# First phase of a two-block transformer kernel: an embedding chunk's split ahead of the pair sums, shift rows around the sum of squares, latents' weights taken earlier

## What is computed

```python
mod = c_act @ w_ada[l] + b_ada[l]
shift, scale, gate = jnp.split(mod, 3, axis=-1)
h = rms_norm(x) * (1.0 + scale[:, None, :]) + shift[:, None, :]
proj = h @ w_in[l]
xr, gr, qc, kvc, kr, ga = jnp.split(proj, split_points(IN_SPLITS), axis=-1)
...
x = x + jax.nn.sigmoid(x @ w_ple_gate[l]) * (p[l] @ w_ple[l])      # second block
```

## Time and profile before

| | us |
|---|---|
| median of 3 runs (lowest to highest) | 2465.32 (2462.7 to 2466.88) |
| the profiled execution | 2466.83 |
| its span, first to last instruction | 2465.3 |
| TensorE busy in it | 2400.5 (97%) |
| VectorE / ScalarE / GpSimd busy | 936.3 / 834.1 / 1001.6 |
| mean granted clock of TensorE | 0.99 |

### The profile page before, as it was taken

One profiled execution on the slowest core, in us unless ns is written; L12 is line 12 of the kernel. 1 busy time (PEld: TensorE's weight loads), 2 busy tenths in 40 slices (PEclk: granted clock), 3 DMA queues, 4 the chain that ended last, 5 costly groups with the idle time before them and its releaser, 6 DMA issues.

```text
span 2465.3 us, 28183 instructions
## 1 busy us (share of the span) xinstructions
PE 2400.5 (97%) x11076; PEld 1902.2 (77%) x11076; DVE 936.3 (38%) x1485; ACT 834.1 (34%) x1283; POOL 1001.6 (41%) x434
## 2 busy tenths in 40 slices
PE   6899999999999999999999999999999999999996
PEld 4567677777888888887787778787878888888885
DVE  7744456566500520210555534343421412202113
ACT  5344444442322432222434333333322312213321
POOL 3344323234455534443332324242434444444553
PEclk8999999999999999999999999999999999999998
DMA  8952133335544343333222323232333444453332
GB/s 322 407 203 79 60 122 109 108 107 188 156 152 141 126 161 96 88 101 90 66 85 61 95 81 107 86 110 83 107 96 101 154 147 129 130 169 119 93 103 85
DMA packets 98579, 309.48 MB, mean 126 GB/s; under 512 B 10640, under 2 KB 12048, under 8 KB 98320
## 3 DMA queue, kind: packets, MB, share of 16 engines
q1 hardware_dynamic: 98448, 307.69, 38.9%
HBM read 285.63 MB, written 20.97 MB: 124 GB/s over the span
## 4 chain that ended last, share of the span: by engine, by line
PE 88%; DVE 5%; ACT 2%; issue 2%; DMA 2%; SPq 1%; POOL 0%; DVEq 0%; ACTq 0%; POOLq 0%
PE bank L539 24%; PE bank L542 24%; PE bank L540 24%; PE bank L535 2%; PE bank L538 2%; PE bank L536 2%; PE bank L1055 2%; PE bank L1079 1%; PE bank L1067 1%; DVE hlo L1756 1%; DMA rawx<-in_wst 1%; PE bank L841 1%; PE bank L852 1%; DVE hlo L2479 1%; PE bank L882 1%
## 5 line engine op out<-in xcount | busy, mean ns | idle before, releaser
L2547 POOL TENSOR_TENSOR wlo<-raw,whi 128x1024 fp32r<-128x1024 f32 x365 | 898.8, 2468 | 1217.3 <-ACT whi L1172 1191.4
L539 PE MATMUL bank<-hhi,whi 128*128 128x512 f32 x2752 | 1087.8, 395 | 14.3 <-DVE hlo L1773 8.1
L542 PE MATMUL bank<-hhi,wlo 128*128 128x512 f32 x2752 | 1078.7, 392 | 23.5 <-POOL wlo L2547 23.4
L540 PE MATMUL bank<-hlo,whi 128*128 128x512 f32 x2752 | 1076.1, 391 | 0.0
L539 PEld LDWEIGHTS bank<-hhi,whi 128*128 128x128 f32 x2752 | 518.4, 188 | 140.0 <-issue 19.4
L542 PEld LDWEIGHTS bank<-hhi,wlo 128*128 128x128 f32 x2752 | 518.5, 188 | 139.7 <-POOL wlo L2547 29.4
L540 PEld LDWEIGHTS bank<-hlo,whi 128*128 128x128 f32 x2752 | 518.7, 188 | 106.9 <-issue 0.7
L1172 ACT ACTIVATE whi<-raw 128x1024 fp32r<-128x1024 f32 x365 | 384.6, 1055 | 589.6 <-PE bank L542 483.9
L2355 DVE TENSOR_SCALAR S<-S,sm 128x512 f32<-128x512 f32 (+1 forms) x64 | 78.1, 1220 | 0.6
L538 PE MATMUL bank<-wlo,hhi 128*128 128x512 f32 x192 | 74.8, 390 | 0.8 <-POOL wlo L2547 0.8
L1621 ACT ACTIVATE S<-S,sm 128x512 f32<-128x512 f32 (+1 forms) x64 | 35.3, 551 | 119.1 <-DVE sm L2345 119.1
(11 more groups left out here) (311 smaller groups left out, 2154.0 us busy)
## 6 DMA issues: line engine op xcount, KB each, us to landing
raw<-in_wst SPq DMA_DIRECT2D x397, 512.0 KB, 3.6
rawx<-in_wst SPq DMA_DIRECT2D x54, 512.0 KB, 8.1
rawy<-in_wst SPq DMA_DIRECT2D x26, 512.0 KB, 4.6
tgs<-TS SPq DMA_DIRECT2D x32, 256.0 KB, 4.1
axr<-tgs SPq DMA_DIRECT2D x32, 256.0 KB, 4.0
X<-in_xt SPq DMA_DIRECT2D x4, 1024.0 KB, 14.4
pls<-stg SPq DMA_DIRECT2D x16, 256.0 KB, 6.5
axr<-in_xt SPq DMA_DIRECT2D x16, 256.0 KB, 2.8
```

What stands on the lines that cost most here:

```text
L539: e.matmul(o, hi, xh, start=first, stop=False)
L540: e.matmul(o, hi, xl, start=False, stop=False)
L542: return e.matmul(o, lo, xh, start=False, stop=last)
L2547: e.tensor_tensor(sub(wlo, PAIR[c], CH), slots[slot(c)], sub(whi, PAIR[c], CH).bitcast(F), ALU.subtract).then_inc(*up("wlo_pool", "wlo", c))
```

## The change

The order in `OPENING` is written anew for the front: the blocks of an embedding chunk are items of their own (`pleb`), the four `ada` chunks of group 0 stand two before and two after the sum of squares, and the first `cols` inside the third embedding chunk. In groups 1 to 7 `cols` comes three units earlier, and two of group 7's units move. A chunk `wq` becomes an item of its own, put in front of the place of its first unit by four chunks of `adt` or `ada`; the splits go one chunk ahead instead of three. GpSimd takes the first two splits before the pair sums. ScalarE makes tiles h after the shift rows of the same group, one tile after the other; VectorE makes the second half of the angles after group 0's scales, and roots x tiles between shift and lower halves. SP loads 22 instead of 19 chunks ahead of the third embedding's stores, and the second part of the constants after the stream's next part.

```diff
--- before.py
+++ after.py
@@ -49,23 +49,33 @@
 
 
 
-    out = [("ple", 0), ("ple", 1), ("xsum",), ("ple", 2)]
-    for e in range(8):
+
+    def rows(e, j):
+        return [("adt", e, j), ("ada", e, j)]
+
+    def blocks(*ns):
+        return [("pleb", n) for n in ns]
+
+    out = [("ple", 0), *blocks(1, 2, 3), ("ple", 1), *blocks(5, 6, 7), *rows(0, 0), *rows(0, 1), ("xsum",),
+           *rows(0, 2), *rows(0, 3), ("ple", 2), *blocks(9), ("cols", 0), *blocks(10, 11),
+           ("ple", 3), *blocks(13, 14, 15)]
+    for e in range(1, 8):
         u = 14 * (e - 1)
         for j in range(4):
-            out.append(("adt", e, j))
-            out.append(("ada", e, j))
-            for _ in range((0, 3, 4, 4)[j] if 0 < e < 7 else (0, 2, 2, 2)[j] if e else 0):
+            out.extend(rows(e, j))
+            for _ in range((0, 3, 4, 1)[j] if e < 7 else (0, 2, 3, 1)[j]):
                 out.append(("unit", u))
                 u += 1
-        if e == 0:
-            out.append(("ple", 3))
         out.append(("cols", e))
-        if e == 0:
-            out.append(("plelast",))
-        else:
-            out.extend(("unit", v) for v in range(u, 14 * e))
+        out.extend(("unit", v) for v in range(u, 14 * e))
     out.extend(("unit", v) for v in range(98, 112))
+    for m in range(14):
+        at = out.index(("unit", 8 * m))
+        ahead = 4
+        while ahead and out[at - 1] != ("pleb", 15):
+            at -= 1
+            ahead -= out[at][0] in ("adt", "ada")
+        out.insert(at, ("wq", m))
     return out
 
 
@@ -98,8 +108,8 @@
             out.append(("ple", item[1], 0))
         elif item[0] in ("adt", "ada"):
             out.append(item)
-        elif item[0] == "unit" and item[1] % 8 == 0:
-            out.append(("wq", item[1] // 8, 0))
+        elif item[0] == "wq":
+            out.append(("wq", item[1], 0))
     blocks("win1", range(23, 25), 2)
     blocks("uq", [4, 5, 0, 1, 2, 3], 1)
     blocks("ukvk", range(4), 1)
...
-NSTART = 1 + max(c for c, w in enumerate(PLAN) if w[0] == "wq")
+NSTART = PLAN.index(("win1", 23, 0))
...
-        return 0 if now["use"] < 2 else 3 if now["use"] < NSTART else LOOK
+        return 0 if now["use"] < 2 else 1 if now["use"] < NSTART else LOOK
...
         elif item[0] == "unit":
-            if item[1] % 8 == 0:
-                begin(c)
             if item[1] % 8 == 7:
                 end(INDEX["wq", item[1] // 8, 0])
+        elif item[0] == "wq":
+            begin(c)
     for c in range(now["use"], len(PLAN)):
...
-                if u % 8 == 0:
-                    wq["c"] = chunk("wq", u // 8, 0)
-                c, hi, lo = wq["c"]
+                c, hi, lo = wq[u // 8]
...
             for item in OPENING:
                 if item[0] == "ple":
-                    embedding(item[1], range(4) if item[1] < 3 else range(2))
-                elif item[0] == "plelast":
-                    embedding(3, range(2, 4))
+                    embedding(item[1], 0)
+                elif item[0] == "pleb":
+                    embedding(*divmod(item[1], 4))
+                elif item[0] == "wq":
+                    wq[item[1]] = chunk("wq", item[1], 0)
...
-                for whole in range(2):
-                    for k in range(2 * g, 2 * g + 2):
+                for k in range(2 * g, 2 * g + 2):
+                    for whole in range(2):
                         w.wait_ge(*done("xr", k))
                         w.wait_ge(*done("adt", INDEX["adt", g, 3]))
...
+            def shift_rows(g):
+                w.wait_ge(*done("used", INDEX["ada", g, 3]))
+                if g >= 2:
+                    w.wait_ge(*done("adacol", g - 2))
+                e.activation(RW[g % 2][:, :], bank("adarow", g)[:, 0:256], ACT.Copy).then_inc(
+                    *up("evac_act", "adacopy", g, frees=("adarow", g)))
+
             for item in OPENING:
-                if item[0] in ("ple", "adt", "ada") or item[0] == "unit" and item[1] % 8 == 0:
+                if item == ("ple", 2):
+                    w.wait_ge(*done("xsum"))
+                    w.wait_ge(*done("eps"))
+                    e.activation(rsx[:, :], bank("xsum")[:, :], ACT.Sqrt, scale=1.0 / 2048, bias=epsc).then_inc(
+                        *up("root_act", "xroot", frees=("xsum",)))
+                    shift_rows(0)
+                if item[0] in ("ple", "adt", "ada", "wq"):
                     use()
                 if item == ("ple", 0):
                     c_tanh(0)
@@ -1258,32 +1280,20 @@
                     x_squares(0, 8)
                     embedding(range(4))
                     x_squares(8, 16)
-                elif item == ("ple", 2):
                     embedding(range(4, 8))
-                    w.wait_ge(*done("xsum"))
-                    w.wait_ge(*done("eps"))
-                    e.activation(rsx[:, :], bank("xsum")[:, :], ACT.Sqrt, scale=1.0 / 2048, bias=epsc).then_inc(
-                        *up("root_act", "xroot", frees=("xsum",)))
-                elif item == ("adt", 0, 0):
+                elif item == ("pleb", 9):
+                    embedding(range(8, 10))
+                elif item == ("pleb", 11):
+                    embedding(range(10, 12))
+                elif item == ("ple", 3):
+                    h_uppers(0)
+                elif item == ("pleb", 15):
+                    embedding(range(12, 16))
+                elif item == ("adt", 1, 0):
                     sines()
-                elif item == ("adt", 0, 2):
-                    embedding(range(8, 12))
-                elif item == ("plelast",):
-                    embedding(range(12, 14))
-                    h_uppers(0)
-                    embedding(range(14, 16))
-                elif item[0] == "adt" and item[1] and item[2] == 0:
-                    if item[1] > 1:
-                        h_uppers(item[1] - 1)
-                elif item[0] == "cols":
-                    g = item[1]
-                    w.wait_ge(*done("used", INDEX["ada", g, 3]))
-                    if g >= 2:
-                        w.wait_ge(*done("adacol", g - 2))
-                    e.activation(RW[g % 2][:, :], bank("adarow", g)[:, 0:256], ACT.Copy).then_inc(
-                        *up("evac_act", "adacopy", g, frees=("adarow", g)))
-                    if g == 7:
-                        h_uppers(7)
+                elif item[0] == "cols" and item[1]:
+                    shift_rows(item[1])
+                    h_uppers(item[1])
 
 
             def x_read():
@@ -1872,26 +1882,27 @@
                 step(hba, V("b_rg_a", 0, 8), 0.5, None, ALU.mult)
                 step(hbx, V("b_rg_x", 0, 8), 0.5, None, ALU.mult, ALU.bypass, "terms")
 
-            def angles():
-                w.wait_ge("pos", 16)
-                e.tensor_copy(PF[:, :], PI32[:, :]).then_inc(*up("term_dve"))
-                step(PF[:, :], PF[:, :], V("invf"), None, ALU.mult)
+            def angles(n):
...
-                    step(KK[:, :], PF[:, :], 1.0 / (2 * np.pi), turn, ALU.mult, ALU.add)
-                    step(KK[:, :], KK[:, :], MAGIC, None, ALU.add)
...
+                        rooted_x(range(2, 4))
+                        h_lowers(0)
+                        rooted_x(range(4, 6))
                     elif g > 1 and j == 0:
                         shifts(g - 1)
-                    elif g > 1 and j == 1:
+                        rooted_x(range(2 * g + 2, min(2 * g + 4, 16)))
                         h_lowers(g - 1)
                     elif (g, j) == (1, 2):
                         w.wait_ge(*done("trig", 0))
                         step(SIN[:, :], SIN[:, :], V("sgn"), None, ALU.mult)
                         T.place["rope",] = T.place.get(("trig", 1), ("vec", 0))
                         T.place["sin",] = now("term_dve")
-                elif item[0] == "cols":
-                    g = item[1]
-                    rooted_x(range(6) if g == 0 else range(2 * g + 4, min(2 * g + 6, 16)))
-                    if g == 0:
-                        shifts(0)
-                        h_lowers(0)
             shifts(7)
             h_lowers(7)
 
@@ -2559,13 +2570,13 @@
                     w.wait_ge(*a)
                 e.tensor_tensor(HT[k][1], src, HT[k][0].bitcast(F), ALU.subtract).then_inc(*up("lo_pool", "hlo", st, k))
 
-            use()
+            use(2)
             for i in range(8):
                 w.wait_ge(*done("xsq", 2 * i))
                 w.wait_ge(*done("xsq", 2 * i + 1))
                 e.tensor_tensor(sqs[i][:, :], sqs[i][:, :], sqt[i % 4][:, :], ALU.add).then_inc(
                     *up("ssum_pool", "xpair", i))
-            use(NSTART - 1)
+            use(NSTART - 2)
             halves(SPLIT_EARLY[turn["use"]])
 
             def latent(which, hi, lo, st):
...
             embedded(0)
             embedded(1)
-            load(19)
+            load(22)
             embedded(2)
             load(24)
             embedded(3)
+            load(INDEX["win1", 24, 1] + 6)
```

(31 more changed lines are left out.)

33 lines of the change are left out of this document (21 added, 12 removed).

## The result

| | before | after |
|---|---|---|
| median, all runs on this chip (lowest to highest) | 2464.15 (2462.7 to 2466.88), 4 runs | 2444.62 (2443.56 to 2446.15), 4 runs |
| the profiled execution, its span | 2466.83, 2465.3 | 2446.15, 2444.4 |
| start of the latents' sum of squares (`sqa`), the phase's end | 179.9 | 156.7 |

The change is 19.5 us faster: ratio 0.992, 95% interval 0.9903 to 0.9937. Forecast was 2441, with a range of 2436 to 2453.

A forecast was written before the change was run, and what follows sets the result against it. The first phase was taken as bound by TensorE's waits on GpSimd's lower weight halves, with queue supply hidden behind. Terms 10.6 + 4.3 + 1.6 - 0.7 + 0 + 6.2 + 3.7 - 0.6 = 25.1 us gave 2441, range 2436 to 2453.

The forecast's parts named there:

- Step 1: Front: with the second embedding chunk split ahead of the pair sums, TensorE ends its products at 23.6 instead of 38.86 us.
- Step 2: Front: the sum of squares starts at 29 instead of 38.86 us, group 1 at 50.5; gain 10.6 us.
- its 56: Upper bound in us for the front's end, if GpSimd stretches VectorE's second half of the angles as before.
- The slow clock, taken at 1.8 us: Front: allowance of 1.8 us for TensorE's lower clock after some 5 us of idle time, slowing the sum of squares.
- Step 3: Latents' chunks four ahead, split one ahead: waits of groups 2, 5, 6 go; gains 6.2 + 3.7 us, group 1 4.3.
- The lateness of `W4` and `W11`: Groups 3 and 7: these splits, queued behind `h_uppers` on ScalarE, come 0.8 to 1.3 us late; losses 0.7 and 0.6.
- Step 4: Columns three units earlier, x tiles rooted between shift and lower halves: `hlo` waits of some 0.3 us go, counted elsewhere.
- Step 5: Load supply: no queue dip at 40 to 60 us, 0.5 us of waiting in group 2, which gains 1.6 us.
- A: Rival: the load supply binds through group 4, so the gain is only 18.9 us, giving 2446; chance 0.17.
- B: Rival: taking chunks ahead does nothing as ScalarE still splits late; only the front's gain stays, 2455; chance 0.13.
- C: Rival: slower, VectorE becomes the bound by sharing with GpSimd, 18.2 us a group, 2474; chance 0.03.
- A VectorE busy above 12 us a group: Sign in the groups of the first phase that was to prove the forecast wrong.

The follow-up runs named there:

- experiment 10: The changed kernel with the sum of squares ahead of `ada` 0,0 and 0,1 on TensorE: 2443.81 us (0.9913).
- experiment 1: The kernel before, with only GpSimd's split of the second embedding chunk moved ahead of the pair sums: 2456.39 us (0.9963).
- experiment 7: The changed kernel with columns and shift rows three units later, where they were before the change: 2443.77 us (0.9915).
- experiment 4: The changed kernel with the second half of the angles, the sines and their sign step behind the last tiles h: 2444.02 us (0.9914).
- experiment 5: As experiment 4, with the third and fourth embeddings' stores behind 36 and 46 loads instead of 22 and 24: 2445.46 us (0.992).
- experiment 11: The changed kernel with all angles behind the last tiles h, blocks 12 to 14 evacuated first, splits three ahead from chunk 80: 2451.57 us (0.9946).
- experiment 12: The changed kernel with all angles behind the last tiles h, blocks 12 to 14 evacuated first, and the sum of squares first: 2452.12 us (0.9946).
- experiment 2: The kernel before, with only the latents' chunks taken four ahead and their splits one ahead of use: 2458.33 us (0.9973).
- experiment 3: The changed kernel without the lead: latents' chunks back at their first unit, splits three ahead: 2451.67 us (0.9947).
- experiment 8: The changed kernel with splits asked three ahead from chunk 80 on; no instruction changed, so another profile of the changed kernel: 2444.55 us (0.9915).
- experiment 9: The changed kernel itself, unedited, measured and profiled a second time: 2444.77 us (0.9915).

## Why the prediction was right, by its steps

**Step 1, right.** The second embedding chunk's products run without a wait to 23.0 (23.6 said), with 0.5 us of waiting in the second profile; moving the split alone gave 12.9 us at group 1's start and 11.6 at the phase's end.

**Step 2, right in size: 10.4 us, 9.2 in the second profile, for 10.6.** The sum started at 29.85 (29 said). The reason was half right: the sum does not set the front, as experiment 10 shows; loads do, and the slow clock behind the waits for them. Nor are two `ada` chunks ahead of the sum what gives the gain: experiment 1, with the old order there, starts group 1 2.6 us earlier than the changed kernel. VectorE's chain (two rooted tiles done at 47) was the risk that the step named with its 56: they were done at 50.2 in the first profile and at 45.9 in the second. The slow clock, taken at 1.8 us, is seen in the sum, which took 8.36 us in the first profile and 9.12 in the second. The stretch of 30 to 40 us of the first:

```profile
30.00:40.00 10.00, 10.00 (x36) 4.46 (x37) 9.39 (x14) 3.76 (x5) 2.79 (x1) 0.88 1.03 407
```

and of the second:

```profile
30.00:40.00 10.00, 10.00 (x32) 4.15 (x32) 9.39 (x14) 2.87 (x3) 2.34 (x1) 0.78 1.03 408
```

**Step 3, the core, right.** Groups 5 and 6 gained 6.5 and 4.1 us (6.2 and 3.7 said). The lateness of `W4` and `W11` (-0.7, -0.6) did not come. I let `h_uppers` end 1 us into the group; ScalarE's timeline has the last one of group 2's tiles end 1 us ahead of group 3's start at 83.0, with the splits right behind:

```profile
81.33 0.80 ACT L1231 ACTIVATE un<-X,sm 128x512 f32<-128x512 f32 x1
82.03 1.04 ACT L1181 ACTIVATE whi<-rawx 128x1024 fp32r<-128x1024 f32 x1
```

GpSimd's half is done at 86.4, before the fifth unit at 87.7. Columns three units earlier moved the tiles too, which that term left out. It was too large besides: in experiment 7, with the columns late, the tiles do end 1.1 us into group 3, and GpSimd's half is done at 85.5, when the fifth unit's product with it is due at 85.6. Groups 3 and 7 gained 0.4 and 0.6 us instead of losing 1.3.

**Step 4, no term.** Experiment 7 puts it at 0.4 us in each of groups 3 to 6, and has group 2 shorter without it.

**Step 5, the term that was mis-sized.** No dip came, and the stall of group 2 for a load was foreseen, but at 0.5 us. It is 2.1 us in the second profile, and the slow clock behind it (0.90) makes group 2 16.7 us for 13.7: a loss of 1.3 against before, where 1.6 of gain stood. The step's formula had the awaited chunk (number 26, the second `ada` of group 2) land at 64.7; TensorE got it at 67.6. By the rates of that profile (365 GB/s to 40 us, 412 to 52, 410 after) some 25.9 MB had moved by then, an estimate, where the formula counts 24.8 up to that landing. What the 1.1 MB between them are no view shows; transfers already under way behind the chunk would be such. In the first profile group 2 costs the same by another way: group 1 gained 1.6 of the 4.3 said, since VectorE met two splits. Groups 1 and 2 together: 32.3 and 29.6 us, 27.2 said. Experiments 4 and 5 show the order of the limits: VectorE in some executions, then the queue. The slow clock that step 3 takes away elsewhere came back here, and step 5 had no term for it.

**The sum.** 25.1 said at the phase's end; 23.2 and 24.4 measured. That it is so near is partly luck, since misses of opposite sign cancel: by the table the front and groups 1 and 2 took 0.3 and 5.1 us more than said (1.5 and 2.4 in the second profile), groups 3 to 7 took 3.6 us less (3.3). By medians the change is 19.5 us; 1.2 of the 5.6 that are missing come from the kernel before, whose median moved from 2465.32 to 2464.15 with a fourth run. The rest of the program, from there to the span's end, took 2285.4 us before and 2287.7 and 2287.9 after. Over all profiles but those of experiments 11 and 12 it lies from 2285.4 to 2288.4 without a pattern, so a single profile cannot say whether these 2 us are the change's. One piece is seen: a wait of 0.67 us for `wlo` at 161.4. It is in experiments 4 and 7 too, whose rest is 2285.4 and 2285.5, so it doesn't make the 2 us. That stays open.

**The rivals.** A (supply through group 4, 2446) is half true, and the measured time, 2444.62, lies nearer to it than to the forecast: in the second profile the queue binds in group 2 and costs 3.9 us there (16.7 for 12.8), where A's price was 6. Groups 3 to 6 never wait for it. B is refuted by experiments 2 and 3. C has the right mechanism, VectorE stretched by GpSimd; VectorE was busy 14.4 of 16.1 us in group 1, and it held groups 1 and 2 only, far from its price.

**A sign that was badly chosen.** A VectorE busy above 12 us a group was to prove the forecast wrong. It was busy 14.4 us in group 1 and 12.4 in group 2, and the forecast held: busy time alone does not say that an engine is late. Rows 1 had 14.47 in group 1 before the change. The other signs did not come: no wait of 1.5 us on `wlo` behind the front, and group 1 began at 50.8, before 54.

## What to carry to other kernels

When a wait has its cause in another engine's order, find the instruction that the late one is queued behind: here one split gave 11.6 us alone and a lead of four chunks 10.4, nearly as much as the whole edit, and both could be priced from the stretches that never waited. Then ask what the freed time runs into: the earlier front made another split late (experiment 1), and each further edit of it only handed the wait from VectorE to the queue and back. An operation moved off a busy engine to a quiet place still needs cover on the engine that consumes it. And take a second profile of the same program before a difference of 1 or 2 us in one stage is given a cause.

## What the runs showed of the hardware that was not expected

- Two VectorE operations that take 0.89 us together, and two that take 1.29, took 2.96 and 3.49 us when a GpSimd split began during them; the reciprocal (3.35 us) was not stretched. Which case comes was decided by 1.2 us in the start of a split. The same instructions ended the phase at 156.7 in the first case and at 155.5 in the two profiles of the second (experiments 8 and 9).
- It was the execution with the slower clock at 30 to 40 us (the sum of squares 9.12 us for 8.36) that ended the phase earlier: ScalarE's half of the split, which stands behind the root of that sum, came 1.2 us later (40.78 for 39.55), and GpSimd's half fell under the reciprocal.
